# Scaling the attention probabilities of the first stack before they are turned, instead of scaling the attention output

## The reference

```python
def hybrid_layer(x, ...):
    h = rmsnorm(x, norm_g)
    proj = einsum("bsd,de->bse", h, w_in)      # 14 groups of 256 columns
    y_a = conformer_conv(a_u, a_v, ...) * silu(a_z)       # 31 taps, layer norm
    y_b = short_gated_conv(b_b, b_c, b_x, ...) * silu(b_z)
    y_c = window_gqa(c_q, c_k, c_v, sink) * silu(c_z)     # 4 heads of 64
    y_d = neighborhood_attn(d_q, d_k, d_v, rpb) * silu(d_z)
    return x + einsum("bse,ed->bsd", concatenate([y_a, y_b, y_c, y_d]), w_out)
```

## Time and profile before

| | before |
|---|---|
| median of 3 runs | 1271.8 us (1271.57 to 1273.4) |
| the profiled execution, its own time | 1271.64 us |
| span of the profile | 1269.8 us |
| PE busy | 1260.5 us, 99% of the span |
| DVE busy | 986.7 us, 78% |
| ACT busy | 697.5 us, 55% |
| POOL busy | 270.0 us, 21% |
| granted PE clock | 0.999 |

### The profile page before, as it was taken

How to read it: one execution, slowest core, us unless ns; L and a number is a source line. 1 busy time by engine, 2 the same in 40 slices (tenths; PEclk the granted TensorE clock), 3 DMA queues, 4 the chain that set the end, 5 groups by cost and what they waited for, 6 DMA issues and landing times.

```text
span 1269.8 us, 21116 instructions
## 1 busy us (share of the span) xinstructions
PE 1260.5 (99%) x7986; PEld 1124.0 (89%) x7986; DVE 986.7 (78%) x1187; ACT 697.5 (55%) x929; POOL 270.0 (21%) x258
## 2 busy tenths in 40 slices
PE   9999999999999999999999999999999999999998
PEld 8998999888888899988888888888889998888886
DVE  6999789898767679868767778767676986877676
ACT  6674567465444586836444455444458673644444
POOL 2763275283000113201000009100011420100000
PEclk9999999999999999999999999999999999999999
DMA  9854654647666554346666655766654535566661
GB/s 281 257 183 166 202 147 150 180 146 222 198 189 187 156 165 144 128 141 185 196 184 185 198 166 176 214 182 190 198 161 138 166 134 150 177 189 197 193 186 52
DMA packets 281359, 224.02 MB, mean 176 GB/s; under 512 B 25996, under 2 KB 264234, under 8 KB 281288
## 3 DMA queue, kind: packets, MB, share of 16 engines
q1 hardware_dynamic: 279144, 220.23, 57.5%
q10 hardware_dynamic: 2032, 2.67, 0.6%
q0 software_dynamic: 112, 0.15, 0.0%
HBM read 221.85 MB, written 3.14 MB: 177 GB/s over the span
## 4 chain that ended last, share of the span: by engine, by line
PE 90%; DVE 6%; ACT 2%; issue 2%; DMA 0%; POOLq 0%; SPq 0%; DVEq 0%; POOL 0%; ACTq 0%
PE wide L1692 26%; PE wide L1695 13%; PE big L1659 9%; PE big L1660 9%; PE big L1661 8%; PE wide L1659 6%; PE wide L1660 6%; PE wide L1661 6%; DVE w_lo L936 2%; PE wide L1811 1%; PE big L1716 1%; PE big L1800 1%; PE big L1786 1%; DVE work L1345 1%; PE wide L1981 1%
## 5 line engine op out<-in xcount | busy, mean ns | idle before, releaser
L936 DVE TENSOR_TENSOR w_lo<-w_raw,w_hi 128x2048 fp32r<-128x2048 f32 x203 | 475.0, 2342 | 94.5 <-ACT w_hi L512 90.2
L512 ACT ACTIVATE w_hi<-w_raw 128x2048 fp32r<-128x2048 f32 x204 | 389.6, 1911 | 165.0 <-PE big L1661 125.2
L1692 PE MATMUL wide<-h_both,w_hi 128*128 128x512 f32 x1408 | 356.7, 393 | 0.0
L1692 PEld LDWEIGHTS wide<-h_both,w_hi 128*128 128x128 f32 x1408 | 254.6, 189 | 48.5 <-DVE h_both L951 2.0
L1659 PE MATMUL wide<-h_both,w_hi 128*128 128x256 f32 x736 | 213.6, 290 | 0.3 <-DVE h_both L951 0.3
L1660 PE MATMUL wide<-h_both,w_hi 128*128 128x256 f32 x736 | 208.1, 283 | 0.0
L1661 PE MATMUL wide<-h_both,w_lo 128*128 128x256 f32 x736 | 208.1, 283 | 0.0
L1695 PEld LDWEIGHTS wide<-h_both,w_lo 128*128 128x128 f32 x1408 | 194.2, 190 | 15.0
L1695 PE MATMUL wide<-h_both,w_lo 128*128 128x256 f32 x1408 | 198.8, 282 | 0.0
L1659 PE MATMUL big<-w_hi,y_hi 128*128 128x512 f32 x480 | 189.1, 394 | 0.0
L1660 PE MATMUL big<-w_lo,y_hi 128*128 128x512 f32 x480 | 187.3, 390 | 0.0
(11 more groups left out here) (254 smaller groups left out, 1459.1 us busy)
## 6 DMA issues: line engine op xcount, KB each, us to landing
w_raw<-in_w_in SPq DMA_DIRECT2D x112, 512.0 KB, 4.7
w_raw<-in_ffn_w_gate SPq DMA_DIRECT2D x88, 512.0 KB, 4.0
w_raw<-in_ffn_w_up SPq DMA_DIRECT2D x88, 512.0 KB, 5.2
w_raw<-in_ffn_w_down SPq DMA_DIRECT2D x88, 512.0 KB, 4.1
w_raw<-in_w_out SPq DMA_DIRECT2D x32, 512.0 KB, 4.3
work<-rpb_shifted SPq DMA_DIRECT2D x32, 64.0 KB, 3.4
rpb_shifted<-rpb_rows SPq DMA_DIRECT2D x10, 147.0 KB
x<-in_x SPq DMA_DIRECT2D x2, 512.0 KB, 6.6
```

What stands on the lines that cost most here:

```text
L512: nc.scalar.activation(w_hi[:, r, :], w_raw[:, r, :], ACT.Copy).then_inc(hi_ready, 1)
L936: v.tensor_tensor(w_lo[:, r, :], w_raw[:, r, :], w_hi[:, r, :].bitcast(F32), ALU.subtract).then_inc(lo_ready, 1)
L1692: t_.matmul(o, hi[:, kt, c], h_both[:, kt].rearrange("p a s -> p (a s)"), start=kt == 0, stop=False, skip_group_check=True)
```

## The change

In the first stack:

- `finish(u)` goes from the beginning of DVE's step u + 8 to the end of step u + 7: for unit 0 between the two `split_lo` of step 7, for units 1 and 2 behind `split_lo`, for unit 3 in front of it. After the reciprocals it scales the probabilities of heads 0 and 1 by them, with two operations of 128x256, and counts `heads_scaled`.
- ACT scales heads 2 and 3 with `normalize(u)`, at the beginning of its step u + 8, ahead of `round_hi(u + 11)`. It waits for `inv_ready`.
- `turn_probs` waits for `probs_scaled` and `heads_scaled`, no more for `probs_exp`.
- `spread_inverse` is gone, with its four uses of `aux` in a layer. `gated_y` is one operation from `mix` and the gate instead of two.
- The seven taps of DVE's steps 11 and 12 go to steps 10 and 11.

```diff
-DVE_TAPS_AT = {2: 3, 3: 3, 4: 2, 5: 2, 6: 3, 11: 3, 12: 4}
+DVE_TAPS_AT = {2: 3, 3: 3, 4: 2, 5: 2, 6: 3, 10: 3, 11: 4}
-AUX_1 = 8
+AUX_1 = 4
...
-            def normalize(un, u, keys):
+            def normalize(un, u, heads, keys=S):
                 act.wait_ge(inv_ready, un + u + 1)
                 c = 4 * (u % 2)
-                for h in range(NH):
+                for h in heads:
                     pr = probs[:, u % 2, h * S:h * S + keys]
                     ins = nc.scalar.activation(pr, pr, ACT.Copy, scale=row_inv[:, c + h:c + h + 1])
                 ins.then_inc(probs_scaled, 1)
...
+                    if SC_1 + 1 <= i < SC_1 + 5:
+                        normalize(un, i - SC_1 - 1, (2, 3))
                     round_hi(base, base3, i + RING)
...
-            def finish(un, u, has_sink):
+            def finish(un, u, has_sink, heads=()):
...
                 link(v.reciprocal(row_inv[:, c:c + 4], row_sum[:, c:c + 4]))
                 dve.sem_inc(inv_ready, 1)
+                for h in heads:
+                    pr = probs[:, u % 2, h * S:(h + 1) * S]
+                    ins = v.tensor_scalar(pr, pr, row_inv[:, c + h:c + h + 1], None, ALU.mult)
+                    if h == heads[-1]:
+                        ins.then_inc(heads_scaled, 1)
...
                 def gated_y(u, kt):
-                    n = step_aux()
...
-                    dve.wait_ge(aux_written, n + 1)
-                    v.scalar_tensor_tensor(out=scaled_gate, in0=aux[...], scalar=0.5,
-                                           in1=g[:, :, cols], op0=ALU.mult, op1=ALU.mult).then_inc(aux_read, 1)
-                    dve.wait_ge(aux_read, n + 2)
                     dve.wait_ge(mix_written, un + u + 2)
-                    v.tensor_tensor(yv, mix[...], scaled_gate, ALU.mult).then_inc(mix_read, 1)
+                    v.scalar_tensor_tensor(out=yv, in0=mix[...], scalar=0.5,
+                                           in1=g[:, :, cols], op0=ALU.mult, op1=ALU.mult).then_inc(mix_read, 1)
...
-                    if 0 <= u - 1 < 4:
-                        finish(un, u - 1, u - 1 < 2)
...
                     if i == 7:
                         split_lo(base, 6 + RING)
+                        finish(un, 0, True, (0, 1))
...
+                    if u == 3:
+                        finish(un, u, False, (0, 1))
                     if i != 6:
                         split_lo(base, i + RING)
+                    if u in (1, 2):
+                        finish(un, u, u < 2, (0, 1))
...
             def turn_probs(n, u, keys=S):
+                pe.wait_ge(probs_scaled, n + 1)
                 if n < DEPTH * 4:
-                    pe.wait_ge(probs_exp, n + 1)
-                else:
-                    pe.wait_ge(probs_scaled, n - DEPTH * 4 + 1)
+                    pe.wait_ge(heads_scaled, n + 1)
...
-                    if 0 <= u - 2 < 4:
-                        aux_free()
-                        spread_inverse(l * 4 + u - 2, u - 2, PLAIN if u - 2 < 2 else HORDER)
```

More of the change, by code:

```diff
@@ L320, in stacks_kernel @@
         ho_copied, hn_ready = sem("ho_copied"), sem("hn_ready")
-        inv_ready, probs_scaled = sem("inv_ready"), sem("probs_scaled")
+        inv_ready, probs_scaled, heads_scaled = sem("inv_ready"), sem("probs_scaled"), sem("heads_scaled")
         soft_ready = sem("soft_ready")
@@ L857, in _ @@
                     if SC_2 + 1 <= i < SC_2 + 5:
-                        normalize(un, i - SC_2 - 1, causal_keys(i - SC_2 - 1))
+                        normalize(un, i - SC_2 - 1, range(NH), causal_keys(i - SC_2 - 1))
                     if i != 3:
@@ L1141, in gated_y @@
                     yv = y_f[:, 0:2 * P].rearrange("p (c s) -> p c s", s=P)
-                    scaled_gate = tmp[:, 0:2 * P].rearrange("p (c s) -> p c s", s=P)
-                    dve.wait_ge(aux_written, n + 1)
-                    v.scalar_tensor_tensor(out=scaled_gate, in0=aux[:, 0:2 * P].rearrange("p (c s) -> p c s", s=P), scalar=0.5,
-                                           in1=g[:, :, cols], op0=ALU.mult, op1=ALU.mult).then_inc(aux_read, 1)
-                    dve.wait_ge(aux_read, n + 2)
                     dve.wait_ge(mix_written, un + u + 2)
-                    v.tensor_tensor(yv, mix[:, 0:2 * P].rearrange("p (c s) -> p c s", s=P), scaled_gate, ALU.mult
-                                    ).then_inc(mix_read, 1)
+                    v.scalar_tensor_tensor(out=yv, in0=mix[:, 0:2 * P].rearrange("p (c s) -> p c s", s=P), scalar=0.5,
+                                           in1=g[:, :, cols], op0=ALU.mult, op1=ALU.mult).then_inc(mix_read, 1)
                     dve.wait_ge(mix_read, un + u + 2)
@@ L1813, in values @@
                 ins.then_inc(mix_written, 1)
[L1815 to L1823, removed]
             pe.sem_inc(slot_done, 3)
```

## The result

The changed kernel takes 1276.27 us in the median of 8 runs (1275.9 to 1278.52), the kernel before 1271.92 in 8 runs beside them (1271.57 to 1273.4). The ratio is 1.0033, with a 95% interval of 1.0023 to 1.0043: **slower by 4.3 us**. A gain of 2.5 us was forecast, and the range ended at 1272.0.

A forecast was written before the change was run, and what follows sets the result against it. PE's own work, busy 99% of the span, was taken as the bound: -4.12 + (0.5 + 0.5) + (0.2 + 0.4) = -2.5 us, from 1271.8 to 1269.3 us, range 1267.4 to 1272.0 us.

The forecast's parts named there:

- The gain on PE: Spread of reciprocals removed from PE's list, four times in each of two layers: 4.12 us gained.
- The price of a pair on DVE: DVE's two 128x256 scalings per unit, priced from rows of 350 and 501 ns a piece: p = 0.6 to 1.0 us.
- turn(1) and turn(2): PE's turning of units 1 and 2's probabilities: waits of 0.5 and 0.5 us in the first layer, 0.2 and 0.4 in the second.
- turn(3) and behind: PE's turning of unit 3 and DVE's moved taps before split_lo(14): cost 0, at most 0.3 us; margin under 1.5 us.
- The slow rival: Scaling pairs on DVE locked out by POOL's additions, 6.4 us more on DVE's list: 1275.5 us, chance 6%.
- Its point of decision: The slow rival was to decide once a pair of DVE scalings takes more than about 1.6 us.

The follow-up runs named there:

- no_spread: The kernel before without the spread of reciprocals, with the short gated_y and the first stack's probabilities left unscaled: 1268.6 us, 0.9967.
- two_heads: The changed kernel without DVE's two scalings of each unit, ACT's two kept, two heads left unscaled: 1272.3 us, 1.0000.
- finish3_last: act_all with ACT's exponentials ahead of its last POOL products, PE turning before the eleventh product group, unit 3's reciprocals behind split_lo: 1268.4 us, 0.9970.
- dve_pair_again: finish3_last with heads 0 and 1 scaled on DVE again, as in the change: 1272.95 us, 1.0005.
- act_all: The changed kernel with all four heads scaled on ACT and none on DVE, taps as changed: 1273.2 us, 1.0004.
- after_turn10: The changed kernel with only PE's first-stack turning moved, in front of the eleventh group of products instead of the eighth: 1276.7 us, 1.0039.

## Why the prediction was wrong

- **The gain on PE**, 4.12 us by the rows: 3.6 us by the medians when nothing is paid for it (no_spread), with 4.12 inside the interval. This term was right.
- **The price of a pair on DVE**, p = 0.6 to 1.0 us: 1.40 and 1.35 us beside POOL, 0.62 without, 514 ns for one in the mean of all 16. So it was too small for half of the pairs. The upper row, 501 ns, was a mean of eight operations of 378 to 617 ns, and I took it as the upper end. The share of the total: 3.9 us (two_heads to the changed kernel) or 4.5 us (finish3_last to dve_pair_again).
- **turn(1) and turn(2)**, 0.2 and 0.4 us in the second layer: turn(1) was 0.81 us late against PE's shortened list, and turn(2), at 214.82, 1.08 in all, so 0.27 more. The place was right and turn(1) too small. At turn(1) not ACT's scaling but DVE's own pair ended last: it ended at 205.56, 0.5 us behind ACT's (the row below), and PE turned at 205.66. I had also let ACT's exponentials be ready in time, but DVE stood still for them for 0.50 us, because pt_copy and the products for POOL came first. Line 1210 did get its 0.55 us back, in both places.

```profile
204.15 0.91 ACT L584 ACTIVATE probs<-probs,small 128x256 f32<-128x256 f32 x2 [0.50 <-DVEq L1019]
```

- **The step that failed is "turn(3) and behind"**: "It fits nearly; I take 0" and "Nothing is lost, with a margin under 1.5 us". I priced the moved taps at 0.51 us each, from a place where POOL was idle (row at 103.95), and put them where POOL adds. There they took 3.20 and 3.60 us, 3.2 us more in a layer. The trace of before had this price too: the three taps at 55.36, beside POOL, took 0.9 us each. turn(3) came 0.9 us late. And I followed DVE's lateness only to the next slot's remainder, not to the reader with the least slack. PE was 1.10 us late at the turn back of the layer norm and 2.01 at the last slot of w_out, where DVE's last `y_lo` had 0.3 us to spare before and came 2.3 us late. In the second layer the terms are 0.81, 0.27, 0.92 and 0.06 us up to the convolution's turn and 2.01 behind it, against a forecast of 0.2, 0.4 and nothing more.
- **The slow rival**, at 6%, named DVE's list against POOL as the bound of the stretch. The mechanism was right in part, and its 1275.5 us came near the 1276.3 by some luck: it charged all to the pairs of scalings, which cost 1.5 us in the second layer over their price without POOL, and nothing to the moved taps, which cost 3.2. Its point of decision was not right: a pair needed no 1.6 us, since the taps and the waits for exponentials ate the same margin. I took the margin from DVE's busy time in the stretch (3.3 us free), as if all of that could be filled; but DVE has to stand still where its input isn't there, as in front of the reciprocals of unit 1 (0.50 us).
- **The rule of the Trainium skill** ("SBUF — State Buffer", "Who interferes with whom"), that such operations of DVE and POOL's shut each other out for whole instructions, agrees with the pairs of 1.4 against 0.62 us: the 0.78 us between them are one addition of POOL (two took 1.54 us at 199.23). The taps were slowed as well, but by less than whole instructions: four of them and four additions of POOL ran side by side in 3.7 us, from 227.16 on, and one after another they would take 5.1 us at the prices of each alone. No run takes POOL's additions away, so contention as the cause of the longer times is read from the timelines and not tested by itself.

The cause is settled in its main parts by runs: 3.6 us gained, 3.9 to 4.5 us paid for DVE's scalings, about 2.8 us for ACT's first two heads and the wait on them, and about 0.9 for the moved taps and early reciprocals, mostly the taps. A part of all this was DVE standing still, since the order on ACT and DVE and the later turning, with the same work, brought act_all from 1273.2 to 1268.4 us. These prices hold in the order in which they were measured: they aren't independent of each other.

## What to carry to other kernels

Follow a delay on a helper engine to the reader with the least slack, however many steps behind, and don't stop at the next wait; moving the wait on the bound engine (after_turn10) only shows it somewhere else. Before a wait moves earlier in a list written by hand, look at what the waited engine does just before: here the scaling on the engine with room, the last reciprocals behind one more long operation, exponentials ahead of work that no one was waiting for and a turning 1.1 us later turned a loss of 4.3 us into a gain of 3.5. Price a moved operation from rows with the same neighbours as in its new place.

## What the runs showed of the hardware that was not expected

A tap, an operation of DVE on 128x256 with two inputs in SBUF, took 0.51 us alone and 0.85 to 1.1 us beside POOL's additions. A one-input scaling of the same size took 0.3 us from start to start alone and about 0.7 beside them (0.6 to 0.85 in dve_pair_again). The same 38 operations of the taps' line took 24.4 us before and 30.5 us after, in places with more or less of POOL's work beside them. ACT's copy of the same size with a scale took 0.40 us from start to start in the changed kernel, act_all and finish3_last, with POOL beside it (204.15) and without (213.86).
